# A new table of places for attention's preparation pieces, and a second copy that changes its engine

## The reference, cut to what matters

```
# differential heads (4): two softmax maps per block of queries, rotary on q and k
q = rope(q); k = rope(k)                                    # (heads, 2, l, 32)
s = einsum('bhcqd,bhckd->bhcqk', qi, k) * 32**-0.5
p = softmax(where(mask, s, -1e30))
w = p[:, :, 0] - lam * p[:, :, 1]
o = rmsnorm(einsum('bhqk,bhkv->bhqv', w, v), gain) * (1 - lam_init)

# forgetting heads (4): one map, no rotary, D = cumsum(log sigmoid(fz + bias))
s = einsum('bhqd,bhkd->bhqk', qi, k) * 64**-0.5 + D_q - D_k
o = rmsnorm(einsum('bhqk,bhkv->bhqv', softmax(where(mask, s, -1e30)), v), gain)
```

## Time and profile before

| what | value |
|---|---|
| time, median of 3 runs | 3391.37 us (3385.06 to 3393.1) |
| the profiled execution: its time | 3382.7 us |
| its span (first to last instruction) | 3380.4 us |
| TensorE busy | 3049.2 us, 90% of the span |
| VectorE, ScalarE, GpSimd busy | 1525.9, 828.4, 169.0 us |
| granted TensorE clock, mean | 0.942 of full |

### The profile page before, as it was taken

One profiled execution on the slowest core, in us unless ns is written; L12 is line 12 of the kernel. 1 busy time (PEld: TensorE's weight loads), 2 busy tenths in 40 slices (PEclk: granted clock), 3 DMA queues, 4 the chain that ended last, 5 costly groups with the idle time before them and its releaser, 6 DMA issues.

```text
span 3380.4 us, 44938 instructions
## 1 busy us (share of the span) xinstructions
PE 3049.2 (90%) x16960; PEld 1982.5 (59%) x16960; DVE 1525.9 (45%) x2625; ACT 828.4 (25%) x1917; POOL 169.0 (5%) x239
## 2 busy tenths in 40 slices
PE   8999988898895999999699999888989769999995
PEld 5666556676543555555376665666764345555553
DVE  5666535655325222323366663465553342222325
ACT  4333234432110111111143331344221101111113
POOL 1300000000000000000200000000000000000002
PEclk9999999898996999999899999998989979999996
DMA  5820100001015999999810000000010079999996
GB/s 179 254 58 13 46 13 7 8 16 54 18 44 215 410 409 412 409 410 406 307 56 26 26 26 27 7 13 2 19 51 29 32 303 412 414 418 415 410 411 229
DMA packets 136560, 592.74 MB, mean 175 GB/s; under 512 B 13000, under 2 KB 47816, under 8 KB 119016
## 3 DMA queue, kind: packets, MB, share of 16 engines
q1 hardware_dynamic: 105688, 491.42, 36.9%
q0 software_dynamic: 20400, 72.69, 6.4%
q10 hardware_dynamic: 10336, 26.75, 2.1%
HBM read 524.56 MB, written 66.26 MB: 175 GB/s over the span
## 4 chain that ended last, share of the span: by engine, by line
PE 72%; DVE 15%; ACT 4%; DMA 4%; issue 3%; POOL 1%; SPq 0%; POOLq 0%; PEld 0%; PEldq 0%; ACTq 0%; DVEq 0%
PE ps L1557 7%; PE ps L1563 7%; PE ps L1479 7%; PE ps L1598 6%; PE ps L1125 6%; PE ps L1588 6%; PE ps L1188 6%; PE ps L1615 3%; PE ps L1429 3%; PE ps L1282 3%; PE ps L1243 2%; PE ps L1269 2%; DVE negmax L1866 2%; DMA arena<-w 2%; PE ps L1351 2%
## 5 line engine op out<-in xcount | busy, mean ns | idle before, releaser
L1188 PE MATMUL ps<-arena 128*128 128x260 f32 x1024 | 286.5, 412 | 3.6 <-DVE arena L1799 2.1
L1557 PE MATMUL ps<-arena 128*128 128x512 f32 x544 | 245.8, 605 | 3.2 <-DVE arena L2357 2.0
L1866 DVE TENSOR_REDUCE negmax<-ps 16x1 f32<-16x16 f32 (+8 forms) x216 | 151.2, 704 | 213.6 <-PE ps L1248 211.9
L817 ACT ACTIVATE arena<-ps,negmax 16x16 f32<-16x16 f32 (+8 forms) x216 | 150.8, 698 | 386.0 <-DVE negmax L1866 385.6
L1598 PE MATMUL ps<-arena 128*64 128x256 f32 x2176 | 242.3, 381 | 0.0
L1563 PE MATMUL ps<-arena 128*128 128x256 f32 x1088 | 240.4, 379 | 0.0
L1351 PE MATMUL ps<-arena 128*128 128x256 f32 x1024 | 229.6, 382 | 11.7 <-ACT arena L910 11.7
L1588 PE MATMUL ps<-arena 128*128 128x512 f32 x544 | 239.1, 592 | 0.0
L1563 PEld LDWEIGHTS ps<-arena 128*128 128x128 f32 x1088 | 206.7, 190 | 42.6 <-issue 16.3
L1479 PE MATMUL ps<-arena 128*128 128x512 f32 x512 | 222.4, 592 | 0.0
L1351 PEld LDWEIGHTS ps<-arena 128*128 128x128 f32 x1024 | 191.9, 190 | 46.9 <-ACT arena L910 21.3
(11 more groups left out here) (348 smaller groups left out, 4189.5 us busy)
## 6 DMA issues: line engine op xcount, KB each, us to landing
arena<-w SPq DMA_DIRECT2D x204, 2048.0 KB, 18.6
xg<-arena POOLq DMA_DIRECT2D x51, 512.0 KB, 12.4
xg<-arena ACTq DMA_DIRECT2D x34, 512.0 KB
arena<-w_in SPq DMA_DIRECT2D x16, 1024.0 KB, 6.5
xg<-arena ACTq DMA_DIRECT2D x68, 128.0 KB, 8.9
arena<-w_in SPq DMA_DIRECT2D x16, 512.0 KB, 4.0
arena<-w_out SPq DMA_DIRECT2D x2, 4096.0 KB, 14.0
u_rows<-arena SPq DMA_DIRECT2D x16, 512.0 KB, 2.6
```

Source lines behind the costliest of these rows:

```text
L1188: mm = pe.matmul(out, w_qk[b][:, k, :], uT[:, k, lo:hi], start=(k == 0), stop=(k == KD - 1), skip_group_check=True)
L1557: mm = pe.matmul(ps[:, 0, :], XT[:, c, :], W1[0][:, c, :], start=(c == 0), stop=(c == KD - 1))
L1866: v.tensor_reduce(negmax[0:r, at:at + 1], flat[0:r, side:side + wide_], AX.X, ALU.max, negate=True)\
```

## The change

Two edits. The tables `PLAN_DA` and `PLAN_FX` put the same pieces into other slots, and some into other banks (f0 and e0 exchange banks 2 and 6, e3 goes from 6 to 2, b0 from 6 to 2). In the forgetting heads the copy of bundle 1 (and only that one) goes from VectorE to ScalarE.

```
 PLAN_DA = {
-    1: [[], ["a2.2@1"], ["c1@6"], [], ["d1@2"], ["a2.3@1"]],
+    1: [["a2.2@1", "f0@2"], ["a2.3@1"], [], [], ["c1@6", "d1@2"], []],
-    4: [["e2@6"], ["a3.2@2"], ["f2@6"], ["a3.3@2"], [], ["b3@6"]],
+    4: [["a0.0@2+", "e2@6"], [], [], [], ["b3@6", "f2@6"], ["a0.1@2+"]],
...
# in attend_act
+                    middle = HEADS <= (t - 1) // T < ALL and len(bundles((t - 1) % T)) > 1
...
-                    if parts_ > 1:
+                    if parts_ > 1 or middle:
                         turned(t - 1, 1)
...
# in attend_dve
                     pieces_dve(layer, slot + 3)
-                    if parts_ > 1:
-                        turned(t - 1, 1)
                     pieces_dve(layer, slot + 4)
```

More of the change, by code:

```diff
@@ L156 @@
 PLAN_DA = {
-    0: [["a2.0@1"], ["e0@2"], [], ["f0@6"], ["b1@2"], ["a2.1@1"]],
-    1: [[], ["a2.2@1"], ["c1@6"], [], ["d1@2"], ["a2.3@1"]],
-    2: [["g@4"], ["e1@6"], [], ["f1@2"], ["b2@6"], []],
-    3: [["a3.0@2"], [], ["c2@6"], ["a3.1@2"], ["d2@6"], []],
-    4: [["e2@6"], ["a3.2@2"], ["f2@6"], ["a3.3@2"], [], ["b3@6"]],
[L162 to L165, removed]
-PLAN_FX = {
[L167 to L175, removed]
+    0: [["a2.0@1"], ["b1@2"], ["a2.1@1"], [], ["e0@6"], []],
+    1: [["a2.2@1", "f0@2"], ["a2.3@1"], [], [], ["c1@6", "d1@2"], []],
+    2: [["e1@6", "g@4"], ["f1@2"], [], [], ["b2@6"], []],
+    3: [["a3.0@2", "a3.1@2"], ["c2@6"], [], [], ["a3.2@2", "a3.3@2", "d2@6"], []],
+    4: [["a0.0@2+", "e2@6"], [], [], [], ["b3@6", "f2@6"], ["a0.1@2+"]],
+    5: [["a0.2@2+"], ["a0.3@2+", "o@6"], [], ["c3@6"], [], []],
+    6: [["d3@6"], ["e3@2"], [], ["f3@6"], [], ["h@6"]],
+    7: [[], ["a1.0@6+", "b0@2+"], [], [], [], []],
+    8: [[], ["a1.1@6+", "a1.2@6+", "a1.3@6+", "c0@2+"], [], [], [], ["d0@6+"]]}
+PLAN_FX = {
+    0: [[], [], ["a1.3@2"], [], ["a2.0@6", "a2.1@6"], []],
+    1: [[], [], [], ["a2.2@6"], [], []],
+    2: [["g@2"], [], [], [], ["a2.3@6"], []],
+    3: [[], [], [], [], ["a3.0@2"], []],
+    4: [["a3.1@2"], [], ["a3.2@2"], [], [], []],
+    5: [[], [], ["a3.3@2"], [], [], []],
+    6: [[], [], ["o@6"], [], ["h@6"], []],
+    7: [[], [], ["a0.0@6+", "a0.1@6+"], [], [], []],
+    8: [[], [], ["a0.2@6+", "a0.3@6+", "a1.0@2+"], ["a1.1@2+"], ["a1.2@2+"], []]}
 DURING_V = [[(0, p) for p in now] for now in (
```

## The result

| | before | after |
|---|---|---|
| time, median of 3 runs | 3391.37 us (3385.06 to 3393.1) | 3302.5 us (3292.91 to 3308.63) |
| ratio, with its 95% interval | | 0.974 (0.9716 to 0.9764) |
| span of the profiled execution | 3380.4 us | 3300.7 us |
| TensorE busy | 3049.2 us | 3000.6 us |
| granted clock, mean | 0.942 | 0.957 |

A forecast was written before the change was run, and what follows sets the result against it. TensorE was taken as the bound, standing still about 110 us in both attention layers. Gains of 6.3 + 0.9 + 2.8 = 10.0 us a layer, 20 in both, less 3 for the clock, gave 3366 us; eight-in-ten range 3354 to 3393.

The forecast's parts named there:

- From that I take 3 us for the clock: Both layers: of 20 us gained from waits, 3 us are lost to TensorE's clock, leaving 17 us less.
- rival 1: Tiles 6 and 7, heads 0 and 1: clock falls to 0.61, costing 12 us in all; 3383 us, chance 0.15.
- Rival 4: New waits nearly hidden, at half their values: 6 us more a layer, 3362; with a gaining clock 3355; chance 0.13.
- Rivals 2 and 3: New waits a third bigger, 3382, chance 0.14; VectorE and ScalarE bound tiles 5 to 7, 3402 or 3411, chance 0.10.
- Waits that go, heads 0 to 2: Differential heads: vanishing TensorE waits save 6.8 us each in heads 0 and 1, 4.7 in head 2.
- Waits that come: Differential heads: new waits cost 4.4 us each in heads 0 and 1, 3.2 in head 2; net gain 6.3 a layer.
- Head 3: Tile 4's 0.88 us wait of scores goes, 0.9 gained; the 1.49 and 3.11 at bundle 1 stay, VectorE being late.
- Forgetting heads: Heads 4 to 6: 0.93 us less waiting each, 2.8 for three; the second copy isn't what TensorE waits for.
- the test that I named: Forgetting heads: if they lose more than 5 us, the mechanism is wrong.
- The sum: Attention: 6.3 + 0.9 + 2.8 = 10.0 us a layer, 20 in both, less 3 for the clock: 17 us less.
- The far end of the new waits: Heads 0 to 2, new waits up to 2.00 us: 2.9 lost each in 0 and 1, 1.0 in 2, together 6.8.

The follow-up runs named there:

- after_e3_back: The changed kernel with piece e3 of heads 1 to 3 put back from bank 2 to bank 6; 3319.14 us, ratio 0.9808 to the kernel before.
- the fills: Kernels with useless matmuls or transposes put into TensorE's waits; on the kernel before 3371.63 and 3373.73 us, on the changed kernel 3296.17 and 3295.41 us.
- before_fill_tp2: The kernel before with useless transposes, 12 ahead of c3 and 16 ahead of e3, opening no new sum; 3373.73 us, ratio 0.9944.
- table_only: The kernel before with both new tables, VectorE still making the second copy in the forgetting heads; 3303.34 us, ratio 0.9764.
- copy_only: The kernel before with only the second copy of the forgetting heads moved to ScalarE, old tables kept; 3368.43 us, ratio 0.9959.
- fx_only: The kernel before with only the table PLAN_FX new, VectorE still making the copies; 3358.7 us, ratio 0.9917.

## Why the prediction was wrong, step by step

- **The failed step** is "From that I take 3 us for the clock". In place of 3 us lost, the runs show 46.7 us won. I priced the waits at their own length and thought of the clock as something that only quarters leaving tiles 6 and 7 could change. The sentence of rival 1 that spoke for the truth, "denser work before tile 6, and fewer waits", got no number. Rival 4 had the right sign ("a clock that gains as well") and only 7 us for it.
- **Rival 1** is refuted by its own sign. Head 1's last tiles, for which I feared 0.61, were granted 1.00:

```profile
533.00:556.00 23.00, 19.64 (x140) 14.87 (x140) 15.54 (x30) 12.85 (x34) 0.00 (x0) 1.00 0.00 1
```

  Before, they had 0.77 from c3 on the earlier trace rows. after_e3_back and the fills show the direction: standing still is what lowers the clock there, and quarters may go. The rival's step from the skill's sentence on transposes is refuted too, by before_fill_tp2.
- **Rivals 2 and 3** are out as well: the waits that came were smaller than I took them, not bigger, and before bundle 1 in tile 6 of heads 0 to 2 no wait of 0.2 us or more stands.
- **Waits that go, heads 0 to 2**: right, and a bit more than listed. In head 1 I had 6.8 us; the rows of before that vanish sum to 7.6, since two of 0.22 each went too. c3's wait is nothing now instead of 0.3. Head 0 had a wait of 2.26 where head 1 had 2.00, and four more of 0.39 to 0.85 that I didn't read, of which one is left.
- **Waits that come**: all found, all a little too dear. e1 0.65 for 0.8, f2 0.78 for 1.1, d3 0.60 for 1.0, f3 and h nothing for 0.3, the bundles 0.69 and 0.65 for 0.6 each: 3.4 for 4.4. Net 4.9, 4.2 and 3.6 us in heads 0, 1 and 2 instead of 2.4, 2.4 and 1.5: 12.7 in a layer for 6.3. In head 2 I overlooked that c3 loses its cover: 1.71 became 2.94.
- **Head 3**: 1.7 us for 0.9. The 0.88 is gone as forecast, and with it 0.84 before outputs at the head's start, which I didn't read. The 1.49 and 3.11 that I left standing stay in sum, in other places: 1.79 before bundle 1 in tile 5, then 1.06 before outputs and 1.95 before bundle 1 in tile 6. I blamed VectorE; the rows name ScalarE's copy.
- **Forgetting heads**: 4.0 us of standing still for 2.8. The 0.57 is gone and the 0.96 stays, as forecast; the scores wait 0.73 (0.7), now for ScalarE's copy of a3; the 1.06 of before had no releaser in its row, so the third that I gave to VectorE was a guess that came out. The stage itself is 12.0 us shorter (180.9 to 168.9), the rest of it busy time. I had written that over 5 us would make the mechanism wrong; table_only, with the second copy on VectorE, does as well (161.9 us), so the copy isn't what TensorE waited for, and the test that I named was a bad one.
- **The sum**: 18.3 us of waits in a layer for 10.0, and 22 to 24 us of busy time gained for 1.5 lost to the clock. With every wait at its measured size the sum would have been 37 us; the bigger half of the gain was never in it.
- **Slips without weight**: the forecast of 3366 starts from the profiled execution (3382.7) and the rivals from the median (3391.4); from one base it is 3374. c2 stands behind two quarters, not four. The far end of the new waits leaves out the 0.3 of f3 and h.

## What to carry to other kernels

When TensorE is the bound and a stage has a granted clock below 1.00, price each wait there at about twice its length (here 36.5 us of waits came with 46.7 of busy time), since the busy time around it shrinks too. That is an estimate for a sum of many waits: copy_only gained 6 and 9 us a layer with its waits unchanged, so a single one can come out otherwise. The test is whether the same count of matmuls takes less busy time. Look at length, busy time and granted clock of a window together, never at the waits alone. And a wait that can't be removed can be filled with useless TensorE work, if it opens no new sum in a bank where one is open; here that won 18 to 20 us on the kernel before and perhaps 5 on the one after.

## What the runs showed of the hardware

- Clock: in attention TensorE is busy for 0.87 of the time before and for 0.90 after, and the time at 1.2 GHz halves (85.3 to 37.5 us). The longest single wait that I read in before is 3.11 us.
- The clock doesn't follow the total of the waits alone: copy_only has 54.8 us of standing still against 55.2 and 13.6 us less at the lower level; fx_only has 7.1 less standing still and only 10.2 less. table_only has 23.9 us at the lower level in one layer and 37.5 in the other, with 36.2 and 37.2 of standing still. Which stretches fall shifts with more than the waits, and that stays open.
- Transposes of 128x128 hold the clock as matmuls do (10.2 against 6.8 us at the lower level in heads 0 to 2, from 37.5).
- A copy of 128x512 from PSUM takes 596 ns on ScalarE and 688 on VectorE after the change, as before (687 and 594). Moving the 20 second copies of a layer took 0.4 us off TensorE's standing still in copy_only.
